# Moving 32 modulation tiles out of the first way out and the expert stage, and spreading fetched rows differently over the expert groups

## What is computed

```python
def peer(h, ...):                          # per token: 8 heads x 16 chosen experts of 16384
    act = gelu(einsum('td,thkd->thk', hb, u_tab[idx])) * gate
    return einsum('thk,thkd->td', act, v_tab[idx])

# second block, layer i: six shift/scale/gate vectors for the latents (c) and for the context (c_ctx)
sh1, sc1, gt1, sh2, sc2, gt2 = split(silu(cond) @ w_mod[i] + b_mod[i], 6)
h = x * (1 + sc1) + sh1
x = layer_norm(ALPHA * x + gt1 * mixer(h), ln1_g, ln1_b)
h = x * (1 + sc2) + sh2
x = layer_norm(ALPHA * x + gt2 * conv_ffn(h), ln2_g, ln2_b)
```

## Time and profile before

| | |
|---|---|
| median of three runs | 4272.38 us |
| profiled execution | 4271.25 us, of which the span is 4269.4 us |
| mean granted TensorE clock | 0.959 of full speed |
| busy | PE 92%, PEld 73%, DVE 63%, ACT 33%, POOL 40% of the span |
| chain that ended last | PE 49%, DVE 16%, DMA 7%, issue 4%, ACT 3%, POOL 3% |

### The profile page before, as it was taken

One profiled execution on the slowest core, in us unless ns is written; L12 is line 12 of the kernel. 1 busy time (PEld: TensorE's weight loads), 2 busy tenths in 40 slices (PEclk: granted clock), 3 DMA queues, 4 the chain that ended last, 5 costly groups with the idle time before them and its releaser, 6 DMA issues.

```text
span 4269.4 us, 50376 instructions
## 1 busy us (share of the span) xinstructions
PE 3934.5 (92%) x20059; PEld 3117.5 (73%) x20059; DVE 2683.5 (63%) x4540; ACT 1408.0 (33%) x2382; POOL 1719.8 (40%) x1079
## 2 busy tenths in 40 slices
PE   7888999989777899999999799889999989889998
PEld 4767755437766788888888666778888868656886
DVE  5686655567987888888888435446466630645334
ACT  4212211103584333333333336532222131633222
POOL 3256433104695544444445320033333354444443
PEclk9998999989888999999999899999999989989999
DMA  6210310253237998889888100013344412002331
GB/s 259 67 35 2 123 42 25 104 191 121 94 138 264 326 332 320 325 318 326 326 324 321 55 24 12 16 50 119 99 143 138 134 50 68 7 25 83 95 94 50
DMA packets 199191, 602.75 MB, mean 141 GB/s; under 512 B 17611, under 2 KB 63883, under 8 KB 196524
## 3 DMA queue, kind: packets, MB, share of 16 engines
q1 hardware_dynamic: 149164, 410.03, 27.7%
q0 software_dynamic: 49792, 189.49, 12.1%
HBM read 572.19 MB, written 27.26 MB: 140 GB/s over the span
## 4 chain that ended last, share of the span: by engine, by line
PE 49%; DVE 16%; DMA 7%; issue 4%; ACT 3%; POOL 3%; DVEq 0%; SPq 0%; POOLq 0%; ACTq 0%
PE psum L271 13%; PE psum L273 13%; PE psum L272 13%; PE psum L277 11%; DVE pair L261 4%; DMA selrow<-peerrow,hiU 3%; DMA selrow<-peerv,hiU 2%; DVE selrow L2025 2%; DVE acc L2037 1%; PE psum L372 1%; DMA selrow<-peerrow,row16b 1%; POOL Pe L2909 1%; DVE o L1791 1%; ACT Ah L2091 1%; POOL Pd L2911 1%
## 5 line engine op out<-in xcount | busy, mean ns | idle before, releaser
L250 POOL TENSOR_TENSOR pair<-raw_ring,pair 128x1024 fp32r<-128x1024 f32 x259 | 658.9, 2550 | 1237.4 <-ACT pair L240 1237.3
L240 ACT CAST pair<-raw_ring 128x1024 fp32r<-128x1024 f32 x502 | 512.6, 1047 | 366.4 <-PE psum L273 310.1
L271 PE MATMUL psum<-pfh,pair 128*128 128x352 f32 (+1 forms) x1152 | 387.4, 336 | 22.7 <-DVE Al L2013 15.2
L271 PE MATMUL psum<-ffh,pair 128*128 128x512 f32 (+1 forms) x1056 | 378.9, 359 | 16.5 <-DVE ffl L2224 15.6
L273 PE MATMUL psum<-pfh,pair 128*128 128x352 f32 (+1 forms) x1152 | 383.9, 333 | 0.0
L272 PE MATMUL psum<-pfl,pair 128*128 128x352 f32 (+1 forms) x1152 | 383.3, 333 | 0.0
L273 PE MATMUL psum<-ffh,pair 128*128 128x512 f32 (+1 forms) x1056 | 378.5, 358 | 0.0
L272 PE MATMUL psum<-ffl,pair 128*128 128x512 f32 (+1 forms) x1056 | 378.5, 358 | 0.0
L271 PE MATMUL psum<-pair,Ah 128*128 128x512 f32 (+1 forms) x768 | 306.8, 399 | 21.3 <-DVE pair L261 17.0
L273 PE MATMUL psum<-pair,Al 128*128 128x512 f32 (+1 forms) x768 | 305.5, 398 | 0.0
L272 PE MATMUL psum<-pair,Ah 128*128 128x512 f32 (+1 forms) x768 | 305.0, 397 | 0.0
(11 more groups left out here) (673 smaller groups left out, 9352.3 us busy)
## 6 DMA issues: line engine op xcount, KB each, us to landing
raw_ring<-wmod SPq DMA_DIRECT2D x160, 512.0 KB
raw_ring<-peeru SPq DMA_DIRECT2D x128, 512.0 KB
raw_ring<-peerv SPq DMA_DIRECT2D x128, 512.0 KB
raw_ring<-win SPq DMA_DIRECT2D x48, 512.0 KB
gates<-stage SPq DMA_DIRECT2D x11, 2048.0 KB, 6.9
Gb<-gates SPq DMA_DIRECT2D x32, 704.0 KB
raw_ring<-wgate SPq DMA_DIRECT2D x44, 512.0 KB
raw_ring<-wup SPq DMA_DIRECT2D x44, 512.0 KB
```

The costliest lines, as they stand in the source:

```text
L240: ac.e.copy(self.pair(t)[0], k.R.of(t)).then_inc(*k.A.up("hi", t))
L250: po.e.tensor_tensor(lo, k.R.of(t), hi.bitcast(F), ALU.subtract).then_inc(*k.G.up("lo", t))
L271: e.matmul(out, w[0], x[0], start=first, stop=False, skip_group_check=True)
```

## The change

The silu rows are computed once in the first way out, written to a DRAM buffer `csil` and loaded again where they are needed, without ScalarE. In the way out 16 tiles of modulation are left (2 before the convolution's normalisation, 3 after its second multiplication, 11 among the blocks). The expert stage has none. The even layer's window attention gets 9 (one before the maximum of units 28, 30, ... 44) and its first residual 23: 4, 4, 3, 3, 3, 3, 3 ahead of VectorE's additions for blocks 0 to 6. The bias is added in three pieces, and the gains for the feed-forward (`vector_gains`) are computed before block 7's addition and not at the stage's start. Two rows are fetched in each of groups 0 to 5, and 148 in groups 6 to 30 (23 groups of six, two of five). The two new silu rows and a scratch buffer lie in `Vm`, which the window attention no longer needs; SyncE's ring stops after `wqb` until unit 23 is done, loads them, and goes on.

```diff
-MODS_OUT = ((8,), (9,), (10,), (11,), (12,), (13,), (14, 15, 16, 17, 18, 19), (20, 21, 22, 23))
+MODS_OUT = ((5,), (6,), (7,), (8,), (9,), (10,), (11, 12, 13), (14, 15))
...
+def biased(k, dv, a, b):
+    m, bias = k.mods2[0][:, a:b, :], k.vec["bmod2"][:, a:b]
+    dv.e.tensor_tensor(m, m, bc(bias, 2, [128, b - a, 2]), ALU.add).then_inc(*k.V.up())
 
...
-    for j in range(6):
+    for j in range(2):
         modulated(k, dv, j, k.crow2a, k.junk2a, A.at("crow2a", 1))
...
+        if n == 1:
+            for j in range(2, 5):
+                modulated(k, dv, j, k.crow2a, k.junk2a)
     step(26)
     step(27)
-    modulated(k, dv, 6, k.crow2a, k.junk2a)
-    modulated(k, dv, 7, k.crow2a, k.junk2a)
...
+    po.wait_ge(k.A.at("crow2a", 1))
+    for i in range(2):
+        po.e.dma_start(k.d["csil"][i], k.crow2a[i]).then_inc(*k.csave.up())
...
-MODS = {20 + 4 * i: 24 + i for i in range(24)}
...
+def u_rows(gi):
+
+    return 2 * gi if gi < 6 else 12 + (ROWS_OF - 12) * (gi - 6) // (GROUPS - 6)
+
+
 def chosen_rows(gi):
 
     if gi < GROUPS:
-        return list(range(ROWS_OF * gi // GROUPS, ROWS_OF * (gi + 1) // GROUPS))
+        return list(range(u_rows(gi), u_rows(gi + 1)))
...
-            if t in MODS:
-                modulated(k, dv, MODS[t], k.crow2b, k.junk2b, A.at("crow2b", 1))
...
-        for i in range(2 if gi == 4 else 0):
-            ac.wait_ge(k.crow[3 + i].at())
-            e.activation(k.crow2b[i], k.crow2b[i], AF.Silu).then_inc(*A.up("crow2b", i))
...
-            dv.wait_ge(k.R.at(("wmod2", 1, s, j)), A.at("crow2c", 1 - s))
+            dv.wait_ge(k.R.at(("wmod2", 1, s, j)), k.crow[3].at(2 - s))
...
+        meanwhile(j)
...
-        e.dma_start(f.crow, k.d["crow"][2]).then_inc(*k.crow[5].up())
+        e.dma_start(f.crow, k.d["csil"][1]).then_inc(*k.crow[3].up())
...
+MODS_EVEN = {28 + 2 * i: j for i, j in enumerate((16, 17, 18, 19, 20, 21, 22, 23, 40))}
+MODS_RES = [j for j in range(24, 40)] + [41, 42, 43, 44, 45, 46, 47]
+
+
+def beside(j):
+
+    return MODS_RES[3 * j + min(j, 2):3 * j + 3 + min(j + 1, 2)] if j < 7 else []
...
+    def between(i):
+        if next_head(i):
+            prepare(next_head(i))
+        if i in MODS_EVEN:
+            dv.wait_ge(k.cev[0].at(), k.cev[1].at())
+            modulated(k, dv, MODS_EVEN[i], f.crow, f.junk)
+
+    vector_attend(k, dv, f.at, between)
     V.name("end", "evat")
     everyone(k, dv, "evat")
     e.tensor_tensor(k.sel, k.sq["ident"][:, 0:1], k.sq["ident"][:, 64:65], ALU.add).then_inc(*V.up())
-    vector_gains(k, dv, "ff0", m, 24, SEG2, k.vec["ln1g"][:, 0:8], k.vec["ln1b"][:, 0:8])
-    vector_residual(k, dv, "res0", "about", m, 16, SEG2, True)
+    dv.wait_ge(V.now())
+    biased(k, dv, 16, 24)
+    dv.wait_ge(V.now())
+
+    def while_projected(j):
+        for t in beside(j):
+            modulated(k, dv, t, f.crow, f.junk)
+        if j == 7:
+            dv.wait_ge(V.now())
+            biased(k, dv, 24, 48)
+            dv.wait_ge(V.now())
+            vector_gains(k, dv, "ff0", m, 24, SEG2, k.vec["ln1g"][:, 0:8], k.vec["ln1b"][:, 0:8])
+
+    vector_residual(k, dv, "res0", "about", m, 16, SEG2, True, while_projected)
...
+        for n in (0, 1) if t == 4 else (2, 3, 4) if t == 5 else ():
+            raw(("wmod2", 0, n), d["wmod2"][n])
...
-        for n in range(6) if t == 3 else (6, 7) if t == 6 else ():
-            raw(("wmod2", 0, n), d["wmod2"][n])
...
+    for j in MODS_EVEN.values():
+        raw(("wmod2", 0, j), d["wmod2"][j])
...
+        for j in beside(t[0][1]) if t[0][0] == "about" else ():
+            raw(("wmod2", 0, j), d["wmod2"][j])
...
+    R.load(sp, ("wqb", 7))
+    sp.wait_ge(k.P.at("eva", "o", 23), k.csave.at(2))
+    for i in range(2):
+        e.dma_start(k.ev.crow[i], k.d["csil"][i]).then_inc(*k.cev[i].up())
```

More of the change, by code:

```diff
@@ L1525, in lay_peer @@
     k.Ah, k.Al = [m.rounded("Ah", DENSE) for _ in range(4)], [m.rounded("Al", DENSE) for _ in range(4)]
-    at3 = m.at
-    k.junk2b = m.take("junk", 1024)
-    m.at = at3
     k.gl, k.pr = [m.take("gl", DENSE) for _ in range(3)], [m.take("pr", DENSE) for _ in range(3)]
@@ L1531, in lay_peer @@
     k.acc = m.take("acc", 1024)
-    both = m.at
     k.tok = [m.take("tok", 1024) for _ in range(3)] + [k.acc]
@@ L1536, in lay_peer @@
     assert m.at <= at2 - 776 - 128
-    m.at = both
-    k.crow2b = [m.take("crow", 1024)]
-    m.at += 1216
-    k.crow2b.append(m.take("crow", 1024))
     m.at = low + 4096
@@ L1657, in vector_route @@
     everyone(k, dv, "out")
+    dv.wait_ge(k.csave.at(2))
     m, h = k.mod1, k.h
@@ L1809, in scalar_route @@
     everyone(k, ac, "out")
+    ac.wait_ge(k.csave.at(2))
     W.hi(ac, ("wq", 0))
@@ L2057, in vector_experts @@
     dv.wait_ge(V.now())
-    e.tensor_tensor(k.mods2[0], k.mods2[0], bc(k.vec["bmod2"][:, 0:48], 2, [128, 48, 2]), ALU.add).then_inc(*V.up())
+    biased(k, dv, 0, 16)
     dv.wait_ge(V.now())
@@ L2143, in pool_experts @@
         row(s)
-    for i in range(2):
-        e.dma_start(k.crow2b[i], k.d["crow"][1 + i]).then_inc(*k.crow[3 + i].up())
     for n in range(FIRST + len(BESIDE), AHEAD):
@@ L2565, in down @@
             W.hi(ac, ("down", i, j))
-    def crow(n):
-        ac.wait_ge(k.crow[5].at(n + 1))
-        e.activation(f.crow, f.crow, AF.Silu).then_inc(*A.up("crow2c", n))
-    if i == 0:
-        crow(0)
     up(0)
     for gi in range(11):
-        if i == 0 and gi == 4:
-            crow(1)
         if gi < 10:
@@ L2609, in pool_feed @@
             po.wait_ge(k.V.at("mods2", 1, 1, 15))
-            e.dma_start(f.crow, k.d["crow"][1]).then_inc(*k.crow[5].up())
+            e.dma_start(f.crow, k.d["csil"][0]).then_inc(*k.crow[3].up())
         if gi < 10:
@@ L2992, in lay_even @@
     f.four = f.P[1:3] + f.PT[0:2]
+    f.crow, f.junk = [Vm1[:, 1024 * i:1024 * i + 1024] for i in range(2)], Vm1[:, 2048:3072]
+MODS_EVEN = {28 + 2 * i: j for i, j in enumerate((16, 17, 18, 19, 20, 21, 22, 23, 40))}
+MODS_RES = [j for j in range(24, 40)] + [41, 42, 43, 44, 45, 46, 47]
+def beside(j):
+    return MODS_RES[3 * j + min(j, 2):3 * j + 3 + min(j + 1, 2)] if j < 7 else []
 def tensor_rms(k, pe, key, n, sq, mean):
@@ L3699, in load_order @@
             use(("U", n))
-        if 2 * gi in MODS:
-            raw(("wmod2", 0, MODS[2 * gi]), d["wmod2"][MODS[2 * gi]])
         for n in (2 * gi, 2 * gi + 1):
@@ L3848, in count @@
     loads = {n: [Load(s) for s in sems[n]] for n, _ in LOADS}
-    k.cl3, k.xin, k.crow, k.dft, k.stl, k.Gl, k.rowl = (loads[n] for n in ("cl3", "xin", "crow", "dft", "stl", "Gl", "rowl"))
-    k.ktl, k.hkeep, k.ctxl, k.ropel, k.wkvl, k.rope1l, k.outl = (loads[n][0] for n in ("ktl", "hkeep", "ctxl", "ropel", "wkvl", "rope1l", "outl"))
+    k.cl3, k.xin, k.crow, k.cev, k.dft, k.stl, k.Gl, k.rowl = (loads[n] for n in ("cl3", "xin", "crow", "cev", "dft", "stl", "Gl", "rowl"))
+    k.ktl, k.hkeep, k.ctxl, k.ropel, k.wkvl, k.rope1l, k.outl, k.csave = (loads[n][0] for n in ("ktl", "hkeep", "ctxl", "ropel", "wkvl", "rope1l", "outl", "csave"))
     k.consts = [t.at() for t in k.cl3]
@@ L3900 @@
     d["gates"] = nc.dram_tensor("gates", (CHUNKS, 128, 4096), F, kind="Internal").ap()
+    d["csil"] = nc.dram_tensor("csil", (2, 128, 1024), F, kind="Internal").ap()
     d["hkeep"] = nc.dram_tensor("hkeep", (128, 8, 512), F, kind="Internal").ap()
```

5 lines of the change are left out of this document (2 added, 3 removed).

## The result

| | before | after |
|---|---|---|
| median | 4271.24 us (4 runs, 4269.48 to 4278.58) | 4229.41 us (4 runs, 4217.58 to 4231.85) |
| ratio | | 0.9894, 95% interval 0.9878 to 0.9911 |
| span of the profiled execution | 4269.4 us | 4228.4 us |

The change saves 42 us, or 1.1%.

The account below looks back on a forecast made before the run. No engine-wide share was taken to decide; limits were read per stage, mainly TensorE or VectorE. Terms −26 − 27 + 21 − 9 + 4 + 27 = −10 gave 4261 us against the profile, 4262 against the median; range 4236 to 4285.

Parts of the forecast that it names:

- First way out: Way out before the experts: TensorE's stalls, slow products and a late last addition go; −26 us, between −32 and −12.
- The stalls: First way out: TensorE's three waits, for the reciprocal and two `wout` tiles, 15.96 us in all, go.
- the late addition: End of the first way out: the last addition starts 5.0 us after TensorE's end; 3.5 to 4 us saved.
- the slow products: First way out: TensorE's products run slower after a stall; 6.7 us lost, counted as saved.
- Experts 0 to 18: Early expert groups with two fetched rows run at V's 8.34 us on TensorE; −27 us, between −31 and −15.
- Experts 18 to 62: Expert groups mostly of six rows, paced by VectorE with its fetched rows at 17.73 us; +21, between −13 and +56.
- The experts stay with TensorE: Rival, experts 18 to 62: fetched rows come in time, VectorE finishes below 16.03 us; −13 not +21, total 4228; chance 0.14.
- Second pass: Experts' second pass, 1812 to 2346 us: TensorE's waits for `Al` go without modulations; −9 us, between −10 and 0.
- Attention: Window attention: nine modulations of 2.65 us before a maximum that waits for TensorE; +4 us, between 0 and +8.
- First residual: First residual: 23 modulations, slowed by GpSimd's instructions, make VectorE need 96.6 us; +27, between +3 and +35.

Follow-up runs that it names:

- way_out_undone: Changed kernel with the first way out as before and 15 instead of 23 modulations in the first residual; 4226.82 us, 0.9901 of the kernel before.
- traffic_only: Old kernel with the new spread of rows, the experts' 24 modulation tiles loaded but their products replaced by a two-column copy; 4238.67 us.
- more_window: Changed kernel with 20 modulations in the window attention and 12 in the first residual instead of 9 and 23; 4201.74 us.
- vector_lo: Changed kernel with seven of the first residual's nine lower parts computed by VectorE instead of GpSimd; 4217.13 us.
- sums_out: vector_lo with each of GpSimd's five sums of the residual stream cut to 8 of 768 columns (sum then wrong); 4209.26 us.

## Why the prediction was wrong

**First way out, right in sum.** −26 was forecast and −24.2 came; over all profiles with the new order (eight) and the old one (four) the difference of the means is −28. The stalls and the late addition went as named, and way_out_undone brings them back (waits of 5.15 and 6.41 for `wout`). Two terms were mis-sized, and in the sum they offset each other in part. The last two halves were read to end at 956.69, but TensorE does small sum products from 954.85 on, so they took 16.3 and not 18.1, and the addition behind them was 6.7 late and not 5.0. Of the slow products, 3 us are still there in the x96 record.

**Experts 0 to 18, right in kind, 5 us short.** −27 against −32. The groups of two rows ran at 7.6 to 8.7. TensorE was busy without a gap from 1321.8 to 1363, as taken, but the gate products of experts 4 to 14 are 39.1 apart, 7.8 a group, under the 8.34 of V (18 matmuls for each of the two n): by these numbers VectorE gained a lead of 2.6 us on TensorE, and a stretch measured between VectorE's instructions shows it as shorter. The first group of six rows took 12.3, not 14. The cause of the old length stands in the waits of TensorE before (waited for, us in total, times, longest), from expert 0 to 18; its granted clock was 0.89 there, and is 1.00 after:

```profile
PE psum L271 <- DVE pair L261: 18.1, 5, 8.1
```

**Experts 18 to 62, the step that failed.** The prediction said that a group of six rows takes 17.73, "Without the modulation's two instructions" from one group of 20.26, and so +21. Measured is 16.51 a group, −2.7. Three things were wrong in it. First, the wait of 3.14 was the longest of its kind, taken as if it came in every group. The trace of before has 38.7 us over 25 waits, 1.8 a group:

```profile
DVE selrow L2025 <- DMA selrow<-peerrow,hiU: 38.7, 25, 3.1
```

After, with six rows, the mean is 2.0 a group. That is nearly all of the miss: 17.73 − 3.14 = 14.59 us of work was right, and with 2.0 of waits it makes 16.6. Second, the prediction held that the modulation "covered nothing of that wait" and left it there; the wait depended on the tile's transfer beside the fetches, which traffic_only prices at 12.7 us in this stretch. That is the mechanism of the rival "The experts stay with TensorE", which stood at 14 in 100 and 4228. That its 4228 is the measured time is luck: its term was −13 where −2.7 came, and VectorE did not finish below 16.03; other terms made up the rest. Third, the floor was applied to one stretch alone. VectorE did need 10.5 us more than TensorE's 352.7 from 18 to 62, but it had entered that stretch ahead. TensorE waited for only 3.5 of them there:

```profile
PE psum L271 <- DVE Al L2020: 3.5, 3, 1.7
```

From 62 to 124 VectorE caught up again: 489.3 is 7.6 below 31 × 16.03 = 496.9. Over experts 18 to 124 the changed kernel takes 852.4 where TensorE's floor is 849.6; the forecast's +21 − 9 meant 881.

**Second pass, right in kind.** −9 for the waits for `Al` is what came (9.7 to 0.8). The other 5 are VectorE's lateness at expert 62, made good.

**Attention, right within 3.** +1.0 for nine modulations; more_window shows that this price is that of every second unit only.

**First residual, right.** +27.5 for +27, and by the cause named: the excess of the products was priced at 25 and measured 26.4; 2.2 for a lower part is 2.2 by vector_lo, 1.65 for a sum is 1.4 by sums_out. The Trainium skill's rule of the exclusive lock ("SBUF — State Buffer", section "Who interferes with whom") agrees with the trace in kind. In size the rows were nearer: by the rule the prediction had 30.9 us, all of GpSimd's undisturbed time, and VectorE lost 26.4.

So the forecast summed to −10 where −41 came. Of the 31 us between them, 24 lie in one term, 5 in each of its neighbours and 3 in the attention, and the five other rows together came 6 us longer than forecast.
